# RWKV mixer inverse: three levels written out on TensorE in place of a loop, and keys transposed from their own tile in place of a staging tile

## The reference, cut to what matters

```python
def step(state, inp):
    r_t, w_t, k_t, v_t, kk_t, a_t = inp
    sa = jnp.einsum('bhvk,bhk->bhv', state, kk_t)
    state = (state * w_t[:, :, None, :]
             - sa[..., None] * (kk_t * a_t)[:, :, None, :]
             + v_t[..., None] * k_t[:, :, None, :])
    return state, jnp.einsum('bhvk,bhk->bhv', state, r_t)
```

## Time and profile before

| | |
|---|---|
| median of 3 runs | 2129.57 us (2129.04 to 2129.66) |
| the profiled execution's own time | 2129.91 us |
| its span, first to last instruction | 2128.1 us |
| PE busy | 2077.8 us, 98% |
| DVE busy | 1124.0 us, 53% |
| ACT busy | 778.0 us, 37% |
| POOL busy | 165.7 us, 8% |
| mean granted TensorE clock | 0.997 |
| the inverse, from line 836's first matmul to line 942's first | 519.5 to 581.2 us |

### The profile page before, as it was taken

How to read it: one execution, slowest core, us unless ns; L and a number is a source line. 1 busy time by engine, 2 the same in 40 slices (tenths; PEclk the granted TensorE clock), 3 DMA queues, 4 the chain that set the end, 5 groups by cost and what they waited for, 6 DMA issues and landing times. The chain is left out here.

```text
span 2128.1 us, 33196 instructions
## 1 busy us (share of the span) xinstructions
PE 2077.8 (98%) x13332; PEld 1705.0 (80%) x13332; DVE 1124.0 (53%) x1451; ACT 778.0 (37%) x1175; POOL 165.7 (8%) x120
## 2 busy tenths in 40 slices
PE   7999999999799999999999999999999999999998
PEld 6888888777777888888888888877888878888886
DVE  5444444568757444443444443478776675444422
ACT  4332223383434223322322332245665443323221
POOL 2000011002302000011000001101110120000010
PEclk9999999999999999999999999999999999999999
DMA  4222322320012222332222232221111122222321
GB/s 176 93 99 99 111 95 80 104 70 21 23 61 88 100 96 92 113 100 93 80 99 98 91 118 96 80 81 51 51 51 47 56 80 89 99 99 95 113 95 53
DMA packets 48265, 182.65 MB, mean 86 GB/s; under 512 B 6320, under 2 KB 6576, under 8 KB 48048
## 3 DMA queue, kind: packets, MB, share of 16 engines
q1 hardware_dynamic: 48176, 181.39, 24.8%
HBM read 179.27 MB, written 2.10 MB: 85 GB/s over the span
## 5 line engine op out<-in xcount | busy, mean ns | idle before, releaser
L590 PE MATMUL banks<-H,WS 128*128 128x512 f32 x1840 | 730.8, 397 | 11.4 <-DVE H L1997 8.0
L592 PE MATMUL banks<-H,WS 128*128 128x512 f32 x1840 | 717.6, 390 | 0.0
L591 PE MATMUL banks<-H,WS 128*128 128x512 f32 x1840 | 717.5, 390 | 0.0
L1279 ACT ACTIVATE WS<-RAW 128x1024 fp32r<-128x1024 f32 (+1 forms) x308 | 347.1, 1127 | 931.5 <-PE banks L592 928.1
L1913 DVE TENSOR_TENSOR WS<-RAW,WS 128x1024 fp32r<-128x1024 f32 (+1 forms) x308 | 404.4, 1313 | 231.4 <-ACT WS L1279 231.2
L590 PEld LDWEIGHTS banks<-H,WS 128*128 128x128 f32 x1840 | 346.1, 188 | 91.0 <-DVE WS L1913 11.9
L592 PEld LDWEIGHTS banks<-H,WS 128*128 128x128 f32 x1840 | 346.0, 188 | 72.8
L591 PEld LDWEIGHTS banks<-H,WS 128*128 128x128 f32 x1840 | 346.3, 188 | 71.4 <-issue 2.4
L590 PE MATMUL banks<-A,WS 128*128 128x512 f32 x704 | 273.9, 389 | 0.0
L591 PE MATMUL banks<-A,WS 128*128 128x512 f32 x704 | 273.9, 389 | 0.0
L592 PE MATMUL banks<-A,WS 128*128 128x512 f32 x704 | 273.9, 389 | 0.0
(11 more groups left out here) (388 smaller groups left out, 1660.5 us busy)
## 6 DMA issues: line engine op xcount, KB each, us to landing
RAW<-in_w_gate SPq DMA_DIRECT2D x88, 512.0 KB, 3.2
RAW<-in_w_up SPq DMA_DIRECT2D x88, 512.0 KB, 3.2
RAW<-in_w_down SPq DMA_DIRECT2D x64, 704.0 KB, 4.0
RAW<-in_c_in SPq DMA_DIRECT2D x32, 512.0 KB, 3.2
RAW<-in_ab_in SPq DMA_DIRECT2D x22, 512.0 KB, 3.2
RAW<-in_ab_out SPq DMA_DIRECT2D x8, 512.0 KB, 5.6
RAW<-in_c_out SPq DMA_DIRECT2D x8, 512.0 KB, 3.2
X<-in_x SPq DMA_DIRECT2D x4, 512.0 KB, 7.1
```

The costliest lines, as they stand in the source:

```text
L590: pe.matmul(bank[:, :], high[:, cols], upper, start=first and j == 0, stop=False)
L591: pe.matmul(bank[:, :], high[:, cols], lower, start=False, stop=False)
L592: mm = pe.matmul(bank[:, :], low[:, cols], upper, start=False, stop=last and j == len(rows) - 1)
L1279: act.activation(WS[:, 0, c % SPLIT, 0:cols] if dst is None else dst, RAW[:, c % RING, 0:cols], ACT.Copy).then_inc(hi_ready, 1)
```

## The change

On PE the loop over l becomes three written-out levels. The transposition reads block l of KF or AL directly, and its wait for `staged` goes. The six POOL copies, the STAGE tile and the semaphores `staged` and `level_begun` go. The arithmetic is the same.

```diff
@@ pe_level_u, pe_level_xx
-                pe.sem_inc(level_begun, 1)
@@ the middle levels
-                        with pe.Fori(1, 4) as l:
+                        for l in range(1, 4):
                             pe_level_u(q, 1, l)
                             pe_level_xx(q, 0, l)
                             pe.wait_ge(tr_read, l + 4 * q + 4)
-                            pe.wait_ge(staged, l + 3 * q)
-                            pe.sem_inc(level_begun, 1)
-                            tokens_turned(2, STAGE, 0, upper=False, across=q == 0)
+                            tokens_turned(2, (KF, AL)[q], l, upper=False, across=q == 0)
                             pe_level_u(q, 0, l + 1)
                             pe_level_xx(q, 1, l)
@@ POOL
-            def stage(q, l):
...
-                if q or l > 1:
-                    pool.wait_ge(tr_mm, 4 * q + 4 + (l if l > 1 else 0))
-                pool.tensor_copy(STAGE[:, 0, :], (KF, AL)[q][:, l, :]).then_inc(staged, 1)
...
                     fold(0, RF, 3)
                     fold(1, CPRE, 2)
-                    stage(1, 2)
                     fold(1, RF, 3)
-                    stage(1, 3)
```

More of the change, by code:

```diff
@@ L306, in hybrid_trunk_kernel @@
         MKM = [at(f"MKM{b}", TMP_AT + (2 + b) * SEQ, [P, NCHUNK, CHUNK]) for b in range(2)]
-        STAGE = at("STAGE", RAW_AT + 10 * SEQ, [P, 1, SEQ])
         TMPQ = quad("TMPQ", TMP_AT)
@@ L342, in hybrid_trunk_kernel @@
         conv_begun = sem("conv_begun")
-        staged, level_begun = sem("staged"), sem("level_begun")
         z_kept, fold_ready = sem("z_kept"), sem("fold_ready")
@@ L453, in hybrid_trunk_kernel @@
             (ya_ready, 4), (ya_hi, 4), (ya_lo, 4), (z_kept, 14), (p_ready, 14), (low_ready, 2), (low_read, 8), (cum_ready, 2),
-            (exp_ready, 3), (fold_ready, 4), (kk_sq, 4), (ss_max, 4), (bon_in, 4), (bon_mm, 4), (bv_ready, 4), (staged, 6), (level_begun, 34), (fm_ready, 4),
+            (exp_ready, 3), (fold_ready, 4), (kk_sq, 4), (ss_max, 4), (bon_in, 4), (bon_mm, 4), (bv_ready, 4), (fm_ready, 4),
             (tr_mm, 12), (tr_read, 12), (mean_mm, 4), (dev_ready, 4), (g_mm, 4), (sp_act, 2), (sp_vec, 2),
@@ L1848, in _ @@
                         triangle(0, z)
-                    stage(0, 1)
                     for b in range(4):
@@ L1852, in _ @@
                     fold(0, CPRE, 2)
-                    stage(0, 2)
                     branch_lo(0)
                     branch_lo(1)
-                    stage(0, 3)
                     branch_lo(2)
@@ L1860, in _ @@
                         triangle(1, z)
-                    stage(1, 1)
                     fold(0, RF, 3)
                     fold(1, CPRE, 2)
-                    stage(1, 2)
                     fold(1, RF, 3)
-                    stage(1, 3)
                     pool.wait_ge(g_mm, 4)
```

## The result

The changed kernel takes 2133.85 us, the median of 13 runs (2132.37 to 2136.63), against 2129.37 us of the kernel before in 13 runs beside them (2128.22 to 2130.14): a ratio of 1.0021, 95% interval 1.0014 to 1.0029. It is slower by 4.5 us. The forecast was 2134.0 us. The profiled execution took 2134.07 us; its span is 4.2 us longer than before, 2132.3 against 2128.1.

What follows compares the result with a forecast made beforehand. PE ends the kernel; DVE paces its loop, instruction fetching the written-out code. 2129.91 us profiled plus 4.4 for fetching, other parts 0, gives 2134.3, less 0.34 to the median: 2134.0 us, range 2130.0 to 2137.0.

Steps and rivals of the forecast that it cites:

- The kernel is bound by DVE in the loop and by fetching once it is written out: Inverse: DVE sets 3.92 us per loop pass; written-out code waits for instruction packets, 3.79 us each; +4.4 us, chance 0.70.
- listed signs: Packets every 3.5 to 4 us from 534 to 581, five more; stalls 127 matmuls apart; DVE waiting; passes about 4.7 us.
- the clock case: Rival, chance 0.10: longer PE waits drop the clock to 1.2 GHz at last level and recurrence, about +2 us more, 2136.
- Fetch-bound all the way: From the pause at 535.92 to the last group of line 697, PE always waits for packets, straight code of q = 1 included.
- the quickest packets: Two packets in straight code at 554.75 to 561.92, 3.59 us each, taken as the best fetch rate; sum then +2.0 us.
- The POOL copies and the keys' own place, 0: Removing six copies, STAGE and the staged wait, and reading keys directly from KF or AL, gains 0.
- The small instructions, at most 0.5 us and taken as 0: Dropping branch, register instructions and level_begun, some 30 instructions at 15 ns each when fetch-bound, gains at most 0.5 us, counted 0.
- the forecast's range: 2130.0 to 2137.0 us, leaving out most hidden-fetch cases and packets of 4 us or more, together 2 in 10.
- Twelve packets of 3.79 us from the common pause: From the stall at 535.92 in both kernels to line 697's last group at 581.4; line 942 at 585.6, +4.4 us.
- a rival of 0.10: Clock falls to 1.2 GHz as PE stands longer in written-out passes: about +2 us more behind them, 2136 us.
- The rule that fetching is hidden: Trainium skill: next 16 KiB block is fetched while the current runs, so writing out costs 0; hidden rivals: unchanged 0.14, gain 0.06.

Runs made afterwards that it cites:

- e10: Kernel before with PE's loop written out and level_begun removed, POOL copies and their waits kept: 2134.34 us, 1.0025 against before.
- e5: Changed kernel with eight increments of an unused semaphore ahead of each of the 30 written-out groups, 240 in all: 2154.73 us.
- e13: Changed kernel with 34 increments of an unused semaphore at the very start of PE's program, where it waits for input: 2135.31 us.
- e9: Changed kernel with level_begun raised again at the same 34 places, POOL copies still gone: 2138.69 us.
- e4: Kernel before with only q = 1 written out; q = 0 keeps its loop, staging copies and level_begun: 2134.56 us.
- e7: Kernel before with only the first pass of each half written out; the other two stay a loop with staging and level_begun: 2135.88 us.
- e1: Kernel before with PE's loop written out and nothing else; POOL copies, STAGE, waits and level_begun kept: 2138.82 us.
- e3: Kernel before with only q = 0 written out; q = 1 keeps its loop, staging copies and level_begun: 2134.68 us.
- e14: Kernel before with 34 increments of an unused semaphore at the very start of PE's program: 2134.66 us.
- e15: Kernel before with 8 increments of an unused semaphore at the very start of PE's program: 2131.53 us.
- e12: Kernel before with the first 4 of 16 products done twice in the five groups of its loop: 2135.58 us.

## Why the prediction was right, and where its steps were off

*The kernel is bound by DVE in the loop and by fetching once it is written out: shown in the passes.* The packets, stalls and DVE's waits came as listed, five packets more in all. Two of the listed signs came otherwise. The passes were to take about 4.7 us and take 4.9, 6.0 and 4.9 in q = 0 and 5.2, 4.8 and 4.1 in q = 1. And a granted clock under 1 between 535 and 590, named as the sign of the clock case, is there at 546.95.

*Fetch-bound all the way: not so.* From 545.24 to 566.98 no pause is ended by "issue", and the 3.59 us that the forecast read as the quickest packets are, by the groups 0.93 us apart, about PE's own time for that straight code. Such code takes PE about as long as a packet takes to come, and so the sum comes out there without its mechanism; that part is luck.

*The POOL copies and the keys' own place, 0: shown,* e10 against the changed kernel, 0.5 us of 2134.

*The small instructions, at most 0.5 us and taken as 0: wrong in written-out code.* The forecast priced an increment as one instruction to fetch, 15 ns, and counted some 30 small instructions where the increments alone are 34. One costs PE about 0.1 us (e5, e13 with e9, both with some clock in it). By DVE's cadence the loop hid that; written-out code does not. It did no harm to the forecast, since the change both writes out and takes them away: with `level_begun` left in, the time would have been 2138.7, outside the forecast's range.

*Twelve packets of 3.79 us from the common pause: right in kind, with two errors that cancel.* The common pause ended 1.52 us later than in the sum, and over the twelve packets from there the pace was (581.39 - 537.44)/12 = 3.66 us instead of 3.79, 1.5 us less. So the last group came at 581.39, as summed (581.4). That delay came from a fall of the clock at 526.5, ahead of the change; I had a fall of the clock as a rival of 0.10, inside the passes and with its price behind them. Without that fall the shift in a profile is nearer to 3 us: e10's has none at 526 and reaches the recurrence at 584.43, +3.2 us, with a fall at 544.9 in it (it is the fastest of e10's nine executions, 2133.21). The fall at 526.5 is chance between executions: the profiles of e4, e7 and e9 have it too, those of before, e1, e3, e10 and e14 have not, and all are alike up to there. That long pauses make falls likelier is suggested by the profiles. The inverse of the kernel before is at full clock. Falls begin at 546.95 (changed), 544.9 (e10), 541.4 (e14) and 571.0 (e15), among others, each 1.1 to 1.7 us behind the end of a pause of 0.92 to 1.62 us; but e12 has pauses of 1.22 and 1.10 us and none. The spread says little: 4.3 us for the changed kernel, 1.9 for the one before beside it, but 2.5 to 5.0 for the one before in four later rounds of 15 to 23 executions. No run here set the clock by itself, so how much of the 4.5 us is the clock's stays open.

*The rule that fetching is hidden, which the prediction named for its rival: refuted for this code,* by the pauses of 0.35 to 1.34 us at 541.31, 545.24, 570.70 and 574.67. The Trainium skill ("Runtime: NRT & Kernel Launch", Instruction fetch mechanics) also speaks of a window of two such blocks, and of a branch whose target lies outside it forcing a fetch. Here the trace does not agree: the bodies of e14 and e15 (q = 1) lie in three packets, and after the first pass no stall comes; in e14 no packet moves from 537.6 to 545.6.

*What the argument had missed:* it took the kernel before as fixed and the cost as packets times a price. e3, e4 and e7 show that this does not price parts, and e14 and e15 that the same code costs up to 4.8 us more or less by where its boundaries fall. A packet boundary costs only what it delays beyond the next wait that PE has anyway: the second one in a loop's first pass opened 1.0 to 1.6 us (e14, e15), those in the slower straight code 0.4 or nothing. Part of what the change lost is a good position that the kernel before happened to have.

## What to carry to other kernels

Where PE runs many small matmuls, count instructions, not only columns: here 127 matmuls with their weight loads were one packet, it arrived every 3.7 us, and PE could use it up in 1.9 us where 32 matmuls take 0.48, but in 3.7 where they take 0.93. Code of the quick kind belongs in a loop, and the loop's body should meet as few packet boundaries as it can; look in the trace for pauses ended by "issue" in mid-group at equal distances. Before believing a difference of 0.2% between two such kernels, shift one of them by a few instructions at a place where its engine waits anyway, and see whether the difference is larger than that.

## What was not expected of the hardware

- Eight instructions at the start of PE's program move the whole kernel by 1.8 us, 34 by 4.8 us (e15, e14, by the medians, with the falls of the clock that came with it).
- A semaphore increment on PE's own queue costs about 0.1 us in a stream of matmuls: 0.67 to 0.83 us for eight (e5), 3.3 us for 34 (e9 less e13, the clock not parted).
- A loop whose body lies in three packets is not fetched again in its second and third pass (e14, q = 0: no "issue" pause behind 540.28 until the loop ends, and no packet from 537.6 to 545.6).
- The granted clock falls to 1.2 GHz at places that differ between executions of the same code; a pass of the loop that takes 3.92 us took 5.03 (e14) and 5.37 (e15) with it. At 526.5 to 529.9 PE had been busy for 4.8 of the 7 us before it, both in a profile with the fall and in one without.
